# Two more weight places for the expert stage, laid into dead attention buffers, with the gate rows and turned h kept in DRAM

## What is computed

```
merged = sigmoid(gate_a) * (o_mla @ w_o_mla) + sigmoid(gate_b) * (o_fox @ w_o_fox)
x = x + gate_m * (merged @ w_out)
h = rms_norm(x, g_ffn_norm) * (1 + scale_f) + shift_f
scores = sigmoid(h @ w_router)            # 64 experts, top 6 of each token
y_e = (silu(h_e @ w_gate[e]) * (h_e @ w_up[e])) @ w_down[e]     # for each of 64 experts
shared = (silu(h @ w_sh_gate) * (h @ w_sh_up)) @ w_sh_down
out = rms_norm(x + gate_f * (shared + sum of routed y_e), g_final)
```

## Time and profile before

| | us |
|---|---|
| median of three runs | 1056.14 (1056.07 to 1057.98) |
| the profiled execution | 1059.31 |
| its span, first to last instruction | 1057.3 |
| TensorE busy | 1018.6 (96%) |
| VectorE busy | 562.4 (53%) |
| ScalarE busy | 396.1 (37%) |
| POOL busy | 380.5 (36%) |
| moved by DMA | 320.75 MB, mean 303 GB/s |

### The profile page before, as it was taken

One profiled execution on the slowest core, in us unless ns is written; L12 is line 12 of the kernel. 1 busy time (PEld: TensorE's weight loads), 2 busy tenths in 40 slices (PEclk: granted clock), 3 DMA queues, 4 the chain that ended last, 5 costly groups with the idle time before them and its releaser, 6 DMA issues. The chain is left out here.

```text
span 1057.3 us, 14798 instructions
## 1 busy us (share of the span) xinstructions
PE 1018.6 (96%) x5952; PEld 741.1 (70%) x5952; DVE 562.4 (53%) x1022; ACT 396.1 (37%) x680; POOL 380.5 (36%) x309
## 2 busy tenths in 40 slices
PE   8999998999999899999999999999999999999997
PEld 7878886888887687888777565565656565555653
DVE  5899789867766785766667221222222222222243
ACT  5646765556334553657344111121212111111213
POOL 1399999992994069698000000000000000000000
PEclk9999999999999999999999999999999999999999
DMA  9966766477585476555289999999999999999994
GB/s 322 315 220 223 236 219 219 139 244 264 185 254 192 151 250 236 162 174 173 91 255 416 359 415 416 416 416 415 417 416 414 416 415 415 416 417 417 415 416 184
DMA packets 92469, 320.75 MB, mean 303 GB/s; under 512 B 8785, under 2 KB 11889, under 8 KB 75761
## 3 DMA queue, kind: packets, MB, share of 16 engines
q1 hardware_dynamic: 84448, 290.90, 72.1%
q0 software_dynamic: 7664, 28.37, 8.3%
q10 hardware_dynamic: 288, 0.52, 0.1%
HBM read 318.72 MB, written 1.05 MB: 302 GB/s over the span
## 5 line engine op out<-in xcount | busy, mean ns | idle before, releaser
L875 PE MATMUL ps<-hl,L 128*128 128x512 f32 (+1 forms) x1216 | 385.5, 399 | 10.3 <-DVE L L1765 5.6
L875 PEld LDWEIGHTS ps<-hl,L 128*128 128x128 f32 x1216 | 229.1, 192 | 61.0 <-issue 14.6
L1765 DVE TENSOR_TENSOR rlo<-ring,hl 128x1024 fp32r<-128x1024 f32 (+1 forms) x154 | 212.3, 1395 | 79.7 <-ACT hl L1338 79.0
L875 PE MATMUL ps<-rlo,L 128*128 128x512 f32 (+1 forms) x608 | 239.3, 394 | 0.0
L875 PE MATMUL ps<-slots_all,xe 128*64 128x256 f32 x2048 | 230.2, 381 | 1.1 <-DVE rt L2569 1.1
L1338 ACT ACTIVATE hl<-ring 128x1024 fp32r<-128x1024 f32 (+1 forms) x154 | 160.6, 1054 | 129.5 <-PE ps L875 118.4
L875 PEld LDWEIGHTS ps<-slots_all,xe 128*64 128x64 f32 x2048 | 144.8, 137 | 77.1 <-issue 5.1
L864 POOL CAST two<-ident 64x128 fp32r<-64x128 f32 x64 | 18.9, 295 | 480.7 <-PE ps L875 479.3
L818 POOL TENSOR_SCALAR mring<-mring,st 128x512 f32<-128x512 f32 x84 | 173.9, 2071 | 2.0 <-DMA mring<-in_w_mod 0.4
L875 PEld LDWEIGHTS ps<-rlo,L 128*128 128x128 f32 x608 | 116.1, 191 | 24.6
L820 POOL TENSOR_TENSOR macc<-macc,mring 128x512 f32<-128x512 f32 x84 | 121.9, 1452 | 7.0
(11 more groups left out here) (234 smaller groups left out, 915.3 us busy)
## 6 DMA issues: line engine op xcount, KB each, us to landing
slots_all<-in_w_exp_gate SPq DMA_DIRECT2D x64, 1024.0 KB, 22.4
slots_all<-in_w_exp_up SPq DMA_DIRECT2D x64, 1024.0 KB, 22.2
slots_all<-in_w_exp_down SPq DMA_DIRECT2D x62, 1024.0 KB, 22.7
ring<-in_w_in SPq DMA_DIRECT2D x48, 1024.0 KB, 5.5
mring<-in_w_mod POOLq DMA_DIRECT2D x48, 512.0 KB, 4.3
ring<-in_w_out SPq DMA_DIRECT2D x8, 1024.0 KB, 5.2
ring<-in_w_ple_gate SPq DMA_DIRECT2D x4, 1024.0 KB, 6.1
ring<-in_w_branch_a SPq DMA_DIRECT2D x4, 1024.0 KB, 5.5
```

Of the source, the lines that this page charges most:

```text
L875: return e.matmul(o, l, r, start=start, stop=stop)
L1765: return e.tensor_tensor(o, a, b, op)
```

## The change

There are 17 places. Their addresses and their order are written out in `place_at`:

- loads 0 to 5 go into dead attention buffers, and SP issues them between the loads of the dense ring: load 0 behind the load of `of0`, loads 1 and 2 behind the first of `wp0`, loads 3, 4 and 5 behind the first of `wp1`. Each waits for the last reader of the buffer (`emptied`);
- loads 6 to 13 follow the dense ring: `mring`, a ring slot, the two places in L1, and the four other ring slots;
- load 14 goes to a buffer of squares, load 15 into `gbuf`, load 16 into the place where `ht3` lies;
- `shb` is loaded after load 13 and after the last matmul of `wp1`, since it now lies in L0.

The working buffers move the other way, into `hl` and L0: `h3hl`, `yy`, `sh_`, `xp`, `xe`, `shb`. The index of `hl` is turned so that the last four pieces lie in its first four buffers, and `xp` waits for the piece before them. The selectors `pp` go over constants that are no longer used.

Since `gbuf` is given up, POOL writes the gate row (4 KB) to DRAM and later, ahead of its `two` buffer for pair 30, reads it into all partitions (`gate`, 512 KB) where `h3hl` was. `ht3` is written to DRAM (1 MB) after its four parts are ready, and is read back only in the overflow path. `gfin` is now loaded after the last gate and up product.

```
-NE = 15
+NE = 17
...
+        place_at = [X1 + 24 * K, X1, X1 + 40 * K, X1 + 32 * K, X1 + 60 * K, X1 + 68 * K, MR, in_ring[0],
+                    X1 - 16 * K, X1 - 8 * K, *in_ring[1:], X1 + 8 * K, gbuf_at, X1 + 16 * K]
+        early = {first_of["of0"]: (0,), first_of["wp0"]: (1, 2), first_of["wp1"]: (3, 4, 5)}
...
+            def emptied(i):
...
+                elif i == 0:
+                    w.wait_ge(pe_aux.sem, pe_aux.at[("km", 1, 4)])
+                elif i in (1, 2):
+                    w.wait_ge(pe_aux.sem, pe_aux.at[("s2", 7, 1)])
+                elif i == 3:
+                    w.wait_ge(pe_aux.sem, pe_aux.at[("o2", 7)])
+                elif i in (4, 5):
+                    w.wait_ge(pe_aux.sem, pe_aux.at[("omT", 1, 0)])
+                elif i == 6:
+                    w.wait_ge(mac, quarter_done(nq - 1))
+                elif i in (8, 9):
+                    w.wait_ge(pe_w, both(blocks["om1"][-1]))
+                elif i == NE - 3:
+                    w.wait_ge(sq2_a, 4)
+                elif i == NE - 2:
+                    w.wait_ge(*evacuated("wp1", 1))
+                    w.wait_ge(gate_out, 16)
+                elif i == NE - 1:
+                    w.wait_ge(pe_aux.sem, pe_aux.at[("sh", 1)])
+                    w.wait_ge(h_out, 16)
+                else:
+                    freed(last_ring[0 if i == 7 else i - 9])
...
                     e.dma_start(dst, src).then_inc(slot_sem[i % NS], 16)
-            w.wait_ge(pe_aux.sem, pe_aux.at[("km", 1, 4)])
+                for q in early.get(i, ()):
+                    load_expert(q)
+            for i in range(6, NE - 3):
+                load_expert(i)
+            w.wait_ge(pe_w, 2 * npieces)
             e.dma_start(shb[:, :, 0:64], WSG[:, :, 192:256]).then_inc(shared_in, 16)
             e.dma_start(shb[:, :, 64:320], WSU).then_inc(shared_in, 16)
...
+            load_expert(NE - 3)
+            load_expert(NE - 2)
+            for m in range(2):
+                for j0 in (0, 4):
+                    w.wait_ge(*read(("h3T", m, j0)))
+            e.dma_start(kept_h, ht3[:, :, :]).then_inc(h_out, 16)
+            load_expert(NE)
+            load_expert(NE - 1)
+            for i in range(NE + 1, len(loads2)):
+                load_expert(i)
...
+            w.wait_ge(*read(("mod", 11)))
+            e.dma_start(kept_gate.unsqueeze(0), gbuf[0:1, 1, :]).then_inc(gate_out, 16)
             w.wait_ge(pe_w, 2 * npieces)
-            w.wait_ge(*read(("mod", 11)))
             for i in range(NP):
...
+                if i == NP - 2:
+                    w.wait_ge(pe_aux.sem, pe_aux.at[("g", NP // 4 - 1, 7)])
+                    w.wait_ge(gate_out, 16)
+                    e.dma_start(gate[:, :], bass.AP(kept_gate.tensor, 0, [[0, 128], [1, 1024]])).then_inc(gate_in, 16)
...
-            w.wait_ge(pe_aux.sem, pe_aux.at[("g", NP // 4 - 1, 7)])
+            w.wait_ge(pe_aux.sem, pe_aux.at[("gu", NP - 1)])
             e.dma_start(gfin[:, :], row("g_final_2", 1024)).then_inc(gfin_in, 16)
...
                 mine(e.reciprocal(st[:, 70 + m:71 + m], st[:, 68 + m:69 + m]))
                 wait_mine()
+                w.wait_ge(pe_w, both(npieces - 5))
                 tsc(xp[:, m, :], R[:, m, :], st[:, 70 + m:71 + m], None, ALU.mult, None).then_inc(xp_set, 1)
...
             def times_gate(i):
+                w.wait_ge(gate_in, 16)
```

More of the change, by code:

```diff
@@ L97, in two_blocks @@
         ident = place("ident", [128, 128])
+        stri_at = pos[0]
         stri = place("stri", [128, 128])
@@ L101, in two_blocks @@
         cols = place("cols", [128, 80])
+        brd_at = pos[0]
         brd = place("brd", [128, 456])
@@ L112, in two_blocks @@
         gbuf_at = pos[0]
+        kept_gate = nc.dram_tensor("kept_gate", (1024,), F32, kind="Internal").ap()
+        kept_h = nc.dram_tensor("kept_h", (128, 8, 256), F32, kind="Internal").ap()
         gbuf = place("gbuf", [128, 2, 1024])
@@ L147, in two_blocks @@
         assert X0 + 13 * 8192 <= X1
[L148 to L152, removed]
+        MR, HL, XL = X0 + 40 * K, X0 + 48 * K, X0 + 72 * K
+        ht3 = place("ht3", [128, 8, 256], at=X1 + 16 * K)
+        h3hl = place("h3hl", [128, 2, 2, 1024], F32R, at=HL)
+        xe = place("xe", [128, 8, 512], at=XL)
+        yy = place("yy", [128, 2, 1024], F32R, at=HL + 16 * K)
+        sh_ = place("sh_", [128, 2, 768], at=HL + 16 * K)
         hh = place("hh", [128, 3, 256], at=X1 + 48 * K)
@@ L158, in two_blocks @@
         gtt = place("gtt", [128, 2, 2, 64], at=X1 + 59 * K)
[L159 to L175, removed]
+        pp = [place("pp0", [128, 8 * CAP], F32R, at=stri_at), place("pp1", [128, 8 * CAP], F32R, at=brd_at)]
+        slots_all = place("slots_all", [128, (X1 + 76 * K) // 4], at=0)
+        shT = place("shT", [128, 2, 256], at=X1 + 76 * K)
+        assert base + X1 + 78 * K <= nc.sbuf_usable_end
+        gate = place("gate", [128, 1024], at=HL)
+        gfin = place("gfin", [128, 1024], at=XL + 8 * K)
+        yz = place("yz", [128, 2, 1024], F32R, at=HL + 4 * K)
+        yz_plain = place("yz_plain", [128, 2, 1024], at=HL + 4 * K)
+        yy_plain = place("yy_plain", [128, 2, 1024], at=HL + 16 * K)
+        hb = place("hb", [128, 256], at=HL + 12 * K)
+        xp = place("xp", [128, 2, 1024], at=HL + 16 * K)
+        shb = place("shb", [128, 8, 320], at=XL)
+        fb = place("fb", [128, 2, 1024], at=XL)
+        bt = place("bt", [128, 2, 512], at=HL + 12 * K)
+        junk = place("junk", [128, 2, 1024], at=HL + 4 * K)
         PS = [ctx.enter_context(nc.psum_tensor(f"ps{i}", [128, 512], F32)) for i in range(8)]
@@ L321, in hi_of @@
         def hi_of(g):
-            return hl[:, g % NH, 0:2 * pieces[g][2]].rearrange("p (k n) -> p k n", k=2)
-        place2 = [5] + [(len(loads) + q) % NS for q in range(NS)] + [11, 12, 6, 7, 8, 9, *range(13, NE), 10]
+            return hl[:, (g - npieces + 4) % NH, 0:2 * pieces[g][2]].rearrange("p (k n) -> p k n", k=2)
+        last_ring = range(nloads - NS, nloads)
+        in_ring = [X0 + 8192 * (i % NS) for i in last_ring]
+        place_at = [X1 + 24 * K, X1, X1 + 40 * K, X1 + 32 * K, X1 + 60 * K, X1 + 68 * K, MR, in_ring[0],
+                    X1 - 16 * K, X1 - 8 * K, *in_ring[1:], X1 + 8 * K, gbuf_at, X1 + 16 * K]
+        assert len(place_at) == NE
+        first_of = {name: pieces[blocks[name][0]][0] for name in ("of0", "wp0", "wp1")}
+        early = {first_of["of0"]: (0,), first_of["wp0"]: (1, 2), first_of["wp1"]: (3, 4, 5)}
         loads2, at2 = [], {}
@@ L355, in slot2 @@
         def slot2(name):
-            a = place_at[place2[at2[name] % NE]]
+            a = place_at[at2[name] % NE] // 4
             return slots_all[:, a:a + 2048]
@@ L364, in two_blocks @@
         consts_in, x_in, gb_in, gfin_in = (sem(n) for n in ("consts_in", "x_in", "gb_in", "gfin_in"))
+        gate_out, gate_in, h_out, h_in = (sem(n) for n in ("gate_out", "gate_in", "h_out", "h_in"))
         aln_in, wsT_in, p_in, ln_in, up_in = (sem(n) for n in ("aln_in", "wsT_in", "p_in", "ln_in", "up_in"))
@@ L621, in ov_sync @@
         def ov_sync(e):
+            e.dma_start(ht3[:, :, :], kept_h).then_inc(h_in, 16)
             with e.Fori(0, 64) as i:
@@ L634, in ov_tensor @@
             e.wait_ge(ov_bank, 8)
+            e.wait_ge(h_in, 16)
             with e.Fori(0, 64) as i:
@@ L689, in ov_vector @@
                     b = PS[4 + 2 * m + c]
-                    e.tensor_tensor(b[:, :], b[:, :], GATES[:, 1, half(c)], ALU.mult).then_inc(ov_bank, 1)
+                    e.tensor_tensor(b[:, :], b[:, :], gate[:, half(c)], ALU.mult).then_inc(ov_bank, 1)
             e.wait_ge(ov_bank, 12)
@@ L722, in load_beside @@
                     e.dma_start(wkv_up[:, :], D["w_kv_up_2"]).then_inc(up_in, 16)
+            def emptied(i):
+                if i >= NE:
+                    name = loads2_of[i - NE]
+                    if name == "shared":
+                        w.wait_ge(pe_aux.sem, pe_aux.at["router"])
+                    elif name == "sd":
+                        w.wait_ge(sh_pe, 1)
+                    elif name[0] == "d":
+                        w.wait_ge(pe_aux.sem, pe_aux.at[("d", name[1] // 2, 1)])
+                    elif name[0] == "g":
+                        w.wait_ge(pe_aux.sem, pe_aux.at[("gate", name[1] // 2)])
+                    else:
+                        w.wait_ge(pe_aux.sem, pe_aux.at[("gu", name[1] // 2)])
+                elif i == 0:
[18 more added lines that the diff above has]
+                    w.wait_ge(h_out, 16)
+                else:
+                    freed(last_ring[0 if i == 7 else i - 9])
@@ new lines, in load_expert @@
+            def load_expert(i):
+                k, src = loads2[i]
+                name = loads2_of[i]
+                emptied(i)
+                dst = slot2(name)[:, 0:k * src.shape[2]].rearrange("p (a b) -> p a b", a=k)
+                if name[0] == "d" and name[1] >= 62:
+                    dst = slot2(name).rearrange("p (a b) -> p a b", a=2)[:, :, 0:512]
```

(15 more changed lines are left out.)

## The result

The changed kernel takes 1062.07 us (median of 11 runs) against 1056.62 us for the kernel before: a ratio of 1.0047, 95% interval 1.0035 to 1.006. It is slower by about 5 us; 1051.5 was forecast. Its profiled execution took 1061.28 us with a span of 1059.5.

What follows compares the result with a forecast made beforehand. DMA was taken to bound the expert part: first freed place at about 586 us, plus remaining bytes over 416 GB/s. Two places -5.05 and gfin +0.4 sum to -4.65: 1056.14 to 1051.5 us, range 1048.8 to 1055.3.

Steps and rivals of the forecast that it cites:

- shb later: Before the router: shb, issued behind load 13, lands at 565.1, first matmul on it at 568.39; 3.3 us to spare, 0.
- Rival A: Router: shb becomes the wait, landing at 579 in a deep load queue, 10.5 us late; 1062 us, 6%.
- Two more places: Expert part: two loads fewer remain at 586 us, 5.05 us off the DMA stream; -5.05 us.
- B: Rival: TensorE is the bound in the expert part, so the gain ends within 2 us; 1054 to 1056, 9%.
- C: Rival: DMA is also quicker, the whole 8.9 us stall in the expert part goes; 1047.2 us, 6%.
- D: Rival: the places' gain is eaten by the store, the added row and gfin; net -1.3 and less, 1055, 9%.
- Filling by 586: Before the first freed place: all 18 loads land by 586, in time where DMA rests; 0.
- the early loads: Dense part: loads 0 to 5 issued between ring loads delay no ring load, each over 30 us off its use; 0.
- the store: Before 586: writing h (1.05 MB) to DRAM fits in DMA's rest, ending by 580; taken as 0.
- xp: VectorE before the router: xp's wait for the piece before the last four has 2.1 us of cover; 0.
- the gate row: POOL: 4 KB out near 520, 512 KB in near 985, first wanted about 1014; 0.
- gfin late: Last down product: gfin, loaded near 1032, delays the last down halves; +0.4 us, bounds 0 and 1.26.

Runs made afterwards that it cites:

- experiment 1: Changed kernel with the wait split: the first router matmul waits only for the router's weights, shb has its own semaphore; 1052.63 us, ratio 0.9961.
- experiment 2: Kernel before with only the two shb loads moved, after the last matmul of wp1 and the sixth expert load; 1066.38 us, ratio 1.0094.
- Experiment 3: Kernel before with shb loaded late and the router's wait split so that shb has its own; 1059.33 us, ratio 1.0023.
- experiment 8: Changed kernel with unread 512-column matmuls on TensorE ahead of the router's first: 18 of them 1066.33 us, nine of them 1060.74 us.
- experiment 4: Changed kernel with the split wait and 16 places: the place under ht3 unused, h neither stored nor read back; 1056.32 us, ratio 0.9997.
- experiment 5: Changed kernel with the split wait and 17 places, h neither stored nor read back; 1051.86 us, ratio 0.9955.
- experiment 6: Changed kernel with the split wait and 17 places, but loads 0 to 5 issued behind the dense ring; 1062.78 us, ratio 1.0054.

## Why the prediction was wrong

- **shb later: the step that failed.** "So 560.9 + 4.2 = 565.1, and the first matmul on it is at 568.39: 3.3 us to spare, 0." The landing was right to 1 us: forecast 9.4 us after load 13's time, measured 562.8 - 552.5 = 10.3. The need was wrong. I took the first instruction that reads `shb` for the first that waits for it. The wait stands in `route`, on a semaphore that counts three loads, and that matmul stood at 558.28, 10 us earlier. The profile before gave no sign of it: the count was full some 18 us before, and the idle time there was for ScalarE (1.69 us). Experiments 1 and 2 show the step alone, with the new places and without: 9.9 and 9.7 us of router stretch.
- **Rival A** named shb as the wait, and its 1062 is the measured time. That is a coincidence: it comes by a price (a landing at 579) and a place that the runs do not show. It "decides from 568.4 on"; it decides from 558.3. Experiment 3 refutes its queue of 22 us.
- **The clock** was not in the sum at all: a second cost of the same wait. The changed kernel's windows:

```profile
556.00:560.00 4.00, 0.00 (x0) 0.00 (x0) 0.92 (x2) 1.63 (x3) 0.00 (x0) 0.75 1.05 325
560.00:564.00 4.00, 1.19 (x3) 1.04 (x4) 0.00 (x0) 0.00 (x0) 0.00 (x0) 0.50 1.04 397
564.00:568.00 4.00, 4.00 (x14) 3.35 (x14) 0.55 (x2) 0.00 (x0) 0.00 (x0) 0.50 0.54 214
```

  The granted clock falls while TensorE stands (553.4 to 562.8), to 0.50, which is the level of 1.2 GHz, and is 0.97 again from 568 to 572. It cost 2.14 us in this execution; in others it may cost more. Over the 11 runs the mean granted clock and the time go together: six runs at 0.984 to 0.987 took 1058.8 to 1062.1 us, five at 0.980 to 0.982 took 1063.4 to 1064.9. With the wait filled (experiment 8, nine matmuls) the six runs are at 0.987 to 0.991. "TensorE: Matmul & The Clock Gate" of the Trainium skill, section "Part 1: The HAM clock gate", says that the array runs at 1.2 GHz after idling and at 2.4 GHz again once it has been busy; the rows agree, with 0.50 after the stand and 0.97 to 1.00 from 568 on.
- **Two more places: right.** Forecast -5.05, measured -5.15, -5.07 with the split wait, with the weight loads' first wait for a down matrix at 978.4 instead of 852.2. So B, C and D did not come true: the gain neither stopped at 2 us, nor reached 8.9, nor was it eaten up. How the gain divides between the two places is not settled (experiment 4).
- **Filling by 586, the early loads, the store: right,** each put at 0. DMA moved 189 GB/s from 560 to 584. The early loads went out at 462.2, 499.0 and 514.1 to 516.1. No cost of the store stands out of the spread (experiment 5).
- **xp, the gate row: right.** The second xp starts 3.1 us after the write into `rbuf` that its statistics need, in both kernels (559.59 - 556.47, 556.38 - 553.25). The gate row was in 8.7 us after its issue at 989.6, first used at 1015.9.
- **gfin late: right in mechanism,** 0.7 us for 0.4.

Without the failed step the forecast would have been met: 1051.5 against 1052.6 (experiment 1).

## What to carry to other kernels

When a load is moved later, look for the instruction that waits for it, not for the one that reads it: search the semaphore, and ask what else its count holds. A wait that ends long before it is needed leaves no row in a profile, so an old, shared count looks like nothing until one of its loads moves. Give a load that is moved its own semaphore. Space won for prefetching pays by its bytes over the rate of DMA (about 2.5 us for each MB here), as long as DMA rests before the first place comes free.

The kernel to keep is the changed one with the split wait, 1052.6 us (0.9961 of the kernel before), with gfin behind the halves or without: 1052.5.

## What the runs showed of the hardware

- A wait of 8.9 to 9.4 us on TensorE cost 2.1 to 2.7 us more after its end, in the first 6 us of work (the changed kernel, experiments 2 and 8).
- With DMA full for 28 us before it (experiment 6), a 1 MB load landed 18.6 us after its issue, and SP's issue itself took 10.0 us; with DMA 0.65 to 0.80 busy over the 25 us before, it landed after 8.6 to 9.2 us (the changed kernel, experiments 1 and 3).
- A store of 1 MB from SBUF to DRAM landed 3.9 us after its issue when DMA was at rest (the changed kernel) and 10.7 us when it was issued while loads were under way (experiment 1).
